# Small tables loaded already transposed by element-wise transfers, in a one-core hybrid encoder layer

## What is computed

```
mod = jax.nn.silu(c) @ w_ada + b_ada
sh1, sc1, g1, sh2, sc2, g2 = jnp.split(mod[:, None, :], 6, axis=-1)
mix, state = mixer(x * (1.0 + sc1) + sh1)
x = layer_norm(DEEPNORM_ALPHA * x + g1 * mix, ln_g[0], ln_b[0])
ffn = moe_ffn(x * (1.0 + sc2) + sh2, w_router, b_router, w_e_in, b_e_in, w_e_out, b_e_out)
x = layer_norm(DEEPNORM_ALPHA * x + g2 * ffn, ln_g[1], ln_b[1])
```

## Time and profile before

| | |
|---|---|
| three runs, median (lowest to highest) | 1493.74 us (1493.7 to 1495.0) |
| the profiled execution | 1493.7 us, span 1492.0 us |
| mean granted TensorE clock | 0.937 of full speed |
| busy share of the span | TensorE 88%, its weight loads 35%, VectorE 32%, ScalarE 15%, GpSimd 3% |
| moved from and to DRAM | 451.5 MB read, 3.8 MB written |

### The profile page before, as it was taken

The page is one execution under the profiler, slowest core; times in us unless marked ns, Lnnn a source line. Parts: engine busy times, 40 slices in busy tenths (PEclk is TensorE's granted clock), DMA queues, the critical chain, the costliest instruction groups (busy, mean ns, idle before and its releaser), DMA issues.

```text
span 1492.0 us, 20461 instructions
## 1 busy us (share of the span) xinstructions
PE 1315.2 (88%) x7752; PEld 520.1 (35%) x7753; DVE 478.3 (32%) x1190; ACT 218.1 (15%) x446; POOL 47.4 (3%) x78
## 2 busy tenths in 40 slices
PE   4797977719999999999899999999999999999992
PEld 1584333313333333333333333333333333333330
DVE  1383331662232233223322232223323232232237
ACT  0002111031111111110101101120110112112110
POOL 5300000020000000000000000000000000000000
PEclk9897976858999999999999999999999999999996
DMA  9910894338998699999999999959999996835050
GB/s 331 334 39 22 290 305 164 127 110 342 409 410 323 258 410 410 410 409 410 410 410 410 410 410 410 410 224 373 410 410 410 410 410 278 320 137 217 0 190 32
DMA packets 130789, 455.01 MB, mean 305 GB/s; under 512 B 14739, under 2 KB 20765, under 8 KB 130705
## 3 DMA queue, kind: packets, MB, share of 16 engines
q1 hardware_dynamic: 123376, 447.54, 76.9%
q10 hardware_dynamic: 7393, 7.22, 1.6%
HBM read 451.51 MB, written 3.79 MB: 305 GB/s over the span
## 4 chain that ended last, share of the span: by engine, by line
PE 60%; DMA 29%; DVE 5%; issue 3%; ACT 1%; ACTq 1%; SPq 1%; POOL 0%; DVEq 0%; POOLq 0%
DMA w<-in_w_e_out 27%; PE bank L1392 19%; PE bank L1355 19%; PE bank L1314 4%; PE bank L1135 4%; PE bank L1083 3%; PE bank L1267 2%; PE bank L1335 1%; PE bank L1183 1%; PE bank L1186 1%; PE bank L1120 1%; DMA w_odd<-in_w_ada 1%; DMA w<-in_state_conv 1%; PE bank L1377 1%; PE bank L1344 1%
## 5 line engine op out<-in xcount | busy, mean ns | idle before, releaser
L1392 PE MATMUL bank<-w,mt 128*64 128x512 f32 x1216 | 280.2, 615 | 38.7 <-DMA w<-in_w_e_out 38.7
L1355 PE MATMUL bank<-w_even,mt 128*64 128x512 f32 x1344 | 296.5, 594 | 7.9 <-ACT mt L651 7.9
L1355 PE MATMUL bank<-w_odd,mt 128*64 128x512 f32 x1088 | 239.2, 592 | 0.0
L996 DVE TENSOR_SCALAR mt<-bank 128x512 f32<-128x512 f32 x38 | 26.3, 692 | 593.4 <-PE bank L1355 593.4
L1392 PEld LDWEIGHTS bank<-w,mt 128*64 128x64 f32 x1216 | 87.9, 141 | 208.7 <-issue 164.7
L1355 PEld LDWEIGHTS bank<-w_even,mt 128*64 128x64 f32 x1344 | 94.9, 137 | 182.6 <-issue 180.9
L963 DVE TENSOR_TENSOR xy<-bank,xy 128x512 f32<-128x512 f32 (+1 forms) x234 | 146.1, 678 | 8.8 <-PE bank L1314 8.8
L1314 PE MATMUL bank<-mt,gpickT 64*128 64x512 f32 (+1 forms) x468 | 129.6, 631 | 0.7 <-ACT mt L665 0.7
L1355 PEld LDWEIGHTS bank<-w_odd,mt 128*64 128x64 f32 x1088 | 76.2, 137 | 140.2 <-issue 137.7
L1335 PE MATMUL bank<-pick,hb 128*128 128x64 bf16 x1824 | 70.0, 194 | 14.1 <-DVE gpick L991 14.1
L1335 PEld LDWEIGHTS bank<-pick,hb 128*128 128x128 bf16 x1824 | 65.5, 98 | 44.2 <-issue 30.0
(11 more groups left out here) (255 smaller groups left out, 872.5 us busy)
## 6 DMA issues: line engine op xcount, KB each, us to landing
w_even<-in_w_e_in SPq DMA_DIRECT2D x64, 2048.0 KB, 17.5
w<-in_w_e_out SPq DMA_DIRECT2D x64, 2048.0 KB, 18.3
w_odd<-in_w_e_in SPq DMA_DIRECT2D x64, 2048.0 KB, 19.6
w_odd<-in_w_ada SPq DMA_DIRECT2D x12, 2048.0 KB, 8.3
w_even<-in_w_in SPq DMA_DIRECT2D x2, 2048.0 KB, 23.5
w_even<-in_w_in SPq DMA_DIRECT2D x8, 256.0 KB, 5.0
w_even<-in_w_in SPq DMA_DIRECT2D x2, 1024.0 KB, 7.8
w<-in_w_out SPq DMA_DIRECT2D x4, 512.0 KB, 14.6
```

Source lines behind the costliest of these rows:

```text
L996: v.tensor_scalar(glu, bank[1][:, :], LIMIT, None, ALU.min).then_inc(m["glu"], 1)
L1355: ins = mm(bank[bk][64 * h:64 * h + 64, :], xT[:, SLOTS * k:SLOTS * (k + 1)], w1t[:, k, first + 512 * h:first + 512 * (h + 1)], start=Fals ...
L1392: ins = mm(bank[4][64 * h:64 * h + 64, :], aT[:, P * j + SLOTS * (k // 4):P * j + SLOTS * (k // 4) + SLOTS], w2t[:, k, 512 * h:512 * (h + ...
```

## The change

c is loaded directly as `cT` [128, 2, 8], with the model dimension on partitions; the bias tables are loaded as [4, 257] and [8, 32], with the heads on partitions; `conv_b` is loaded as `cbc` [128, 2] with a semaphore of its own. In each of these five transfers neighbouring destination elements are not neighbours in DRAM, so every 4-byte element is a run by itself: 1024 for each c, 1028, 256 and 256. The four TensorE transposes of c and of the tables and the four copies behind them go; GpSimd builds both extended tables from the loaded ones. In ScalarE's queue the two table loads now stand behind the loads of `cs`, `cbc` behind x, and the wait for c with the sigmoid behind the last of the DRAM-to-DRAM copies.

```diff
@@ tiles
-        crow = sb("crow", [2 * DK, P])
-        csil = sb("csil", [2 * DK, P])
+        cT = sb("cT", [P, 2, DK])
-        csig = sb("csig", [2 * DK, P])
+        csig = sb("csig", [P, 2, DK])
-        tabA = sb("tabA", [P, 2, AH])
-        tabB = sb("tabB", [T5_BUCKETS, BH])
-        tabBT = sb("tabBT", [BH, T5_BUCKETS])
+        tabA = sb("tabA", [AH, 2 * A_CLIP + 1])
+        tabB = sb("tabB", [BH, T5_BUCKETS])
+        cbc = sb("cbc", [P, 2])
@@ GpSimd
-            pool.wait_ge(tabB_ready, 1)
+            pool.wait_ge(ld["tabs"], 32)
+            g.tensor_copy(extA[:, 0:256], tabA[:, 0:1].to_broadcast([AH, 256])).then_inc(ext_done, 1)
+            g.tensor_copy(extA[:, 256:512], tabA[:, 0:256]).then_inc(ext_done, 1)
@@ ScalarE's queue
-            eng.dma_start(crow[0:DK, :], c_prompt[0].rearrange("(k p) -> k p", p=P)).then_inc(ld["c"], 16)
-            eng.dma_start(crow[DK:2 * DK, :], c_sample[0].rearrange("(k p) -> k p", p=P)).then_inc(ld["c"], 16)
-            eng.dma_start(tabA[:, :, :], rel_bias_a[0, 0:2 * A_CLIP].rearrange("(t p) h -> p t h", p=P)).then_inc(ld["tabs"], 16)
-            eng.dma_start(tabB[:, :], t5_bias).then_inc(ld["tabs"], 16)
+            eng.dma_start(cT[:, 0, :], c_prompt[0].rearrange("(k p) -> p k", p=P), allow_slow_non_contiguous=True).then_inc(ld["c"], 16)
+            eng.dma_start(cT[:, 1, :], c_sample[0].rearrange("(k p) -> p k", p=P), allow_slow_non_contiguous=True).then_inc(ld["c"], 16)
             eng.wait_ge(cs_zero, 1)
             eng.dma_start(cs[0:CONV_W, :], conv_w[0]).then_inc(ld["cs"], 16)
-            eng.dma_start(cs[CONV_W:CONV_W + 1, :], conv_b[0:1, :]).then_inc(ld["cs"], 16)
             eng.dma_start(cs[32:32 + PADW, :], state_conv[0, 0]).then_inc(ld["cs"], 16)
-            eng.wait_ge(ld["c"], 32)
-            a.activation(csig[:, :], crow[:, :], ACT.Sigmoid).then_inc(csig_done, 1)
+            eng.dma_start(tabA[:, :], rel_bias_a[0].rearrange("r h -> h r"), allow_slow_non_contiguous=True).then_inc(ld["tabs"], 16)
+            eng.dma_start(tabB[:, :], t5_bias.rearrange("r h -> h r"), allow_slow_non_contiguous=True).then_inc(ld["tabs"], 16)
             eng.dma_start(ka_c, cache_a_k[0, 0].rearrange("(t p) h d -> p t (h d)", p=P)).then_inc(ld["ka"], 16)
...
+            eng.dma_start(cbc[:, :], conv_b[0].rearrange("(k p) -> p k", p=P), allow_slow_non_contiguous=True).then_inc(ld["cb"], 16)
...
+            eng.wait_ge(ld["c"], 32)
+            a.activation(csig[:, :, :], cT[:, :, :], ACT.Sigmoid).then_inc(csig_done, 1)
 
             eng.wait_ge(ext_done, 2 + len(t5_runs()))
@@ VectorE
             dve.wait_ge(csig_done, 1)
-            v.tensor_tensor(csil[:, :], crow[:, :], csig[:, :], ALU.mult).then_inc(csil_done, 1)
-            dve.wait_ge(c_turned, 1)
-            v.tensor_copy(scT[:, :, :].rearrange("p k g -> p g k"), bank[4][:, 0:2 * DK].rearrange("p (g k) -> p g k", g=2)).then_inc(scT_done, 1)
-            dve.wait_ge(tabs_turned, 1)
...
+            v.tensor_tensor(scT[:, :, :].rearrange("p k g -> p g k"), cT[:, :, :], csig[:, :, :], ALU.mult).then_inc(scT_done, 1)
@@ TensorE
             pe.wait_ge(consts_done, 2)
-            pe.wait_ge(csil_done, 1)
-            nc.tensor.transpose(bank[4][:, 0:2 * DK], csil[:, :], ident[0:2 * DK, 0:2 * DK]).then_inc(c_turned, 1)
-            pe.wait_ge(ld["tabs"], 32)
-            for t in range(2):
-                nc.tensor.transpose(bank[5][0:AH, P * t:P * (t + 1)], tabA[:, t, :], ident[:, :])
-            nc.tensor.transpose(bank[5][0:BH, 256:256 + T5_BUCKETS], tabB[:, :], ident[0:T5_BUCKETS, 0:T5_BUCKETS]).then_inc(tabs_turned, 1)
-            pe.wait_ge(ld["cs"], 48)
+            pe.wait_ge(ld["cs"], 32)
```

More of the change, by code:

```diff
@@ L189, in hybrid_streaming_encoder_step @@
         ld = {n: sem(f"ld_{n}") for n in (
-            "c", "x", "cs", "ka", "kb", "v", "tabs", "cln", "sinks", "be", "wr", "ext", "toep", "wout",
+            "c", "x", "cs", "ka", "kb", "v", "tabs", "cb", "cln", "sinks", "be", "wr", "ext", "toep", "wout",
             "brow", "final", "x1s")}
@@ L202, in hybrid_streaming_encoder_step @@
             sem(n) for n in ("consts_done", "b3_done", "ext_done", "masks_done", "cs_zero"))
-        csig_done, csil_done, c_turned, scT_done = sem("csig_done"), sem("csil_done"), sem("c_turned"), sem("scT_done")
-        tabs_turned, tabB_ready = sem("tabs_turned"), sem("tabB_ready")
+        csig_done, scT_done = sem("csig_done"), sem("scT_done")
         ada_done, mod_ready = sem("ada_done"), sem("mod_ready")
@@ L420, in _ @@
                    allow_small_or_imprecise_dtypes=True).then_inc(consts_done, 1)
+            extA = MT[0:AH, 0:EXT]
             extB = MT[0:BH, EXT:2 * EXT]
-            pool.wait_ge(tabB_ready, 1)
+            pool.wait_ge(ld["tabs"], 32)
+            g.tensor_copy(extA[:, 0:256], tabA[:, 0:1].to_broadcast([AH, 256])).then_inc(ext_done, 1)
+            g.tensor_copy(extA[:, 256:512], tabA[:, 0:256]).then_inc(ext_done, 1)
             for a, b, bk in t5_runs():
-                g.tensor_copy(extB[:, a:b], tabBT[:, bk:bk + 1].to_broadcast([BH, b - a])).then_inc(ext_done, 1)
+                g.tensor_copy(extB[:, a:b], tabB[:, bk:bk + 1].to_broadcast([BH, b - a])).then_inc(ext_done, 1)
             g.memset(uext[:, :, 0:PADW], 0.0).then_inc(masks_done, 1)
@@ L709, in _ @@
             pv = ps[:, 0:128].rearrange("p (c w) -> p c w", c=2)
-            link(v.tensor_copy(cwT[:, :, :], pv[:, :, 0:32]))
+            link(v.tensor_copy(cwT[:, :, 0:CONV_W], pv[:, :, 0:CONV_W]))
             v.tensor_copy(uext[:, :, U_S:U_S + PADW], pv[:, :, 32:32 + PADW]).then_inc(tr_used, 1)
@@ L757, in _ @@
             dve.wait_ge(masks_done, 1)
+            dve.wait_ge(ld["cb"], 16)
             for c in range(2):
@@ L764, in _ @@
             for c in range(2):
-                link(v.tensor_scalar(yconv[:, c, :], uext[:, c, 0:Y_LEN], cwT[:, c, 0:1], cwT[:, c, CONV_W:CONV_W + 1], ALU.mult, ALU.add))
+                link(v.tensor_scalar(yconv[:, c, :], uext[:, c, 0:Y_LEN], cwT[:, c, 0:1], cbc[:, c:c + 1], ALU.mult, ALU.add))
                 for w in range(1, CONV_W):
```

## The result

| | before | after |
|---|---|---|
| median (lowest to highest) | 1494.25 us (1493.7 to 1495.0), 4 runs | 1511.38 us (1510.74 to 1512.0), 4 runs |
| span of the profiled execution | 1492.0 us | 1511.2 us |
| mean granted TensorE clock | 0.937 | 0.935 |
| DMA packets on ScalarE's queue (q10) | 7393 | 10687 |

The ratio is 1.0114, 95% interval [1.01, 1.0129]: 17.1 us slower, where 1513 was predicted, with 1508 to 1519 as the forecast's own range and 1500 to 1526 for 8 in 10. The bytes moved are the same, 455.01 MB; q10 has 3294 packets more.

What follows compares the result with a forecast made beforehand. Unit 0's start was taken to bound the kernel: hold until 20, 14.5 us of transfers, then sigmoid and product put unit 0 at about 37.5 against 17.50, +20 on 1493.7: 1513.7, say 1513; range 1508 to 1519, 8 in 10 1500 to 1526.

Steps and rivals of the forecast that it cites:

- What sets the start: Start of the kernel: unit 0's start sets everything behind it; a late start isn't caught up in the expert loop.
- The sigmoid's place: ScalarE's queue: sigmoid, at 6.60 before, comes behind all transfers; near 24 by order alone, near 36 in all.
- Depth of about 80 packets per DMA engine: DMA queues: an instruction is held until what was issued before it is down to about 80 packets per engine.
- Spread of `tabA` over four engines: Load of tabA: four rows of 257 elements likely go to four engines, 257 each; evenly spread, 64 each.
- Pace of a packet: Small packets on ScalarE's queue: 19.6 ns apiece alone, taken from 256-byte packets; one for one beside SyncE's unit loads.
- the 281: Small packets left of 338 on the fullest engine after units 0 and 1 load: 5.5 us at 19.6 ns.
- rival of dear packets: Small packets on ScalarE's queue: a 4-byte element costs more than 19.6 ns, +25 us and more; chance 0.23.
- From there to the sigmoid: ScalarE's queue after tabB's issue: 26 transfers take 14.5 us, from 20 to 34.5; sigmoid near 36.1 after its table load.
- VectorE's product: Between sigmoid and unit 0: VectorE's product takes 0.28 us, on the way to unit 0 at about 37.5.
- Unit 0 to unit 3: From unit 0 to unit 3's data: 21.2 us before, taken as even within 1.5 us.
- The clock: Granted TensorE clock, 0.81 in the starting stage: taken as even.
- the end of the hold: ScalarE's queue: one long hold at or behind tabB's issue, ending near 20.

Runs made afterwards that it cites:

- the spread table: Changed kernel with rel_bias_a loaded over 128 partitions in 1024 4-byte elements, tile unused, kind A's biases left out: 1510.09 us, ratio 1.0099.
- the kernel where GpSimd waits: Changed kernel with one more wait: GpSimd begins splitting the expert biases only when scT is done: 1511.78 us, ratio 1.0105.
- the last group: Third of three groups of experiments, each timed beside the kernel before on the same chip; that kernel's median there was 1495.48 us (27 runs).

## Why the prediction was right, step by step

- **What sets the start**: right. Unit 0's start, and behind it units 2, 3 and `w_in`, moved everything; the expert loop gave nothing back.
- **The sigmoid's place**: right, and the largest part. Moved alone it costs 8.3 us.
- **Depth of about 80 packets per DMA engine**: right at the first hold, 82; wrong at the second, which was released with 67 packets left in all, 17 on each of four engines. What the prediction didn't say is where the first hold would stand: at `conv_w`, for 8.86 us. It asked for one hold; there are two.
- **Spread of `tabA` over four engines**: right, shown by the spread table and by the quarter of the pace.
- **Pace of a packet**: the mis-sized term. 19.6 ns was taken from 256-byte packets; 4-byte ones take 11.2 ns at most, and 7.3 to 7.8 where they can be seen by themselves. By 11.2 the 281 take 3.1 us, not 5.5, and with the prediction's own sum the hold would end at 17.5; it ended at 17.8 instead of 20. The agreement is in part chance, since the depth was wrong as well and 0.8 us passed with no packet on q10. The rival of dear packets falls.
- **From there to the sigmoid**: 17.81 to 31.53 is 13.7 us, where 14.5 was taken; the sigmoid began at 32.85 instead of near 36.
- **VectorE's product**: taken at 0.28, it took 1.72 beside GpSimd. This was missed. Unit 0 came at 35.8, 1.7 before the forecast.
- **Unit 0 to unit 3**: taken as even, it gave back 2.2 us (19.05 against 21.2). Why is open. It isn't that x and the others had been moved in the gap: with the sigmoid late in the kernel before they had been too, and there it took 22.1 us (28.59 to 50.68). The traces differ in the Toeplitz reads. In the changed kernel q10 passes nothing from 44 to 50 us, while q1 passes 615 packets; there, from 38 to 48 us, it is 812 beside 814. No run tests this.
- **The clock**: taken as even; in the two profiled executions it was not. The first 6 us of the projections and 7 us in attention, before (from 225) and then after (from 244); the last row is the first 6 us of the projections in the kernel where GpSimd waits. Columns as in the earlier trace rows.

```profile
54.67:60.67 6.00, 6.00 (x18) 4.57 (x19) 0.00 (x0) 0.23 (x1) 0.00 (x0) 0.73 1.14 227
225.00:232.00 7.00, 4.61 (x30) 2.19 (x30) 1.68 (x7) 1.19 (x3) 0.00 (x0) 0.74 1.02 408
```

```profile
70.79:76.79 6.00, 6.00 (x13) 4.24 (x14) 0.00 (x0) 0.00 (x0) 0.00 (x0) 0.51 1.21 262
244.00:251.00 7.00, 4.61 (x24) 2.14 (x22) 1.68 (x7) 1.19 (x3) 0.00 (x0) 0.50 1.03 410
```

```profile
70.94:76.94 6.00, 6.00 (x18) 4.49 (x19) 0.00 (x0) 0.28 (x1) 0.00 (x0) 0.74 1.10 266
```

In the same stretch TensorE is just as busy and gets through fewer instructions, 13 instead of 18 and 24 instead of 30: the granted clock is 0.51 and 0.50 instead of 0.73 and 0.74, the 1.2 GHz of its two levels (1.2 and 2.4) for longer. Before that, while VectorE wrote `hT`, TensorE was busy for less than half of the time in both late kernels (from 62 us to 70.94, 3.81 us in the changed one and 3.53 in the third). The third kernel starts its projections as late as the changed one, at 70.94, and lost nothing. From the second part of the projections (line 1120) to the output projection four other kernels took 142.0 to 142.1 us as the kernel before did, and seven 143.2 to 143.6 as the changed one did, among them all that start sooner than the kernel before. So this term belongs to the execution; that the change causes it isn't shown.

In the profiled executions the output projection is 18.9 us late (268.0 against 249.1) where the projections were 16.1 late. Against +20, three terms were too large (the end of the hold, 20 for 17.8; 14.5 for 13.7; the distance to unit 3, 2.2), and two were missed (the product's 1.4 us and the 2.8 between the two shifts, which go with the clock): 20 - 2.2 - 0.8 - 2.2 + 1.4 + 2.8 = 19.0, about the 19.2 by which the profiled spans differ (1511.2 - 1492.0). The medians differ by 17.1, nearer to the projections' 16.1; the 27 executions of the kernel before in the last group lie 5.2 us apart (1492.69 to 1497.9), so one pair of profiles can't settle 2 us. That the forecast came within 2 us of the median is partly luck, since errors of both signs cancelled.

## To carry to other kernels

Before turning a row load into an element-wise one, count packets, not bytes: on the fullest DMA engine, beside what streams on the other queue, and ask which instruction of the issuing engine is held and what compute stands behind it in program order. Look at the outermost extent of a small load as well: with 4 rows of 257 elements four DMA engines carried it and the queue was held for 6.16 us, with as many elements spread over 128 partitions for 2.02. And a bound found by delaying something is only a bound in that direction: to gain from it, look up the next wait first.

## What the runs showed of the hardware

- Element-wise 4-byte packets pass at 7.3 to 7.8 ns each per DMA engine when the other queue is idle (876 on four engines in 1.6 us, 1633 on sixteen in 0.8), faster than 256-byte ones (19.6 ns), but about one for one with the other queue's packets when it isn't (735 against 813 in 10.88 us).
- A hold behind loads that lie on all 16 engines ended with 71 to 83 packets left on each (82 behind c). Behind the load on four engines it ended with 67 left in all, 17 on each if they lie evenly, after 0.8 us without a packet.
- Holds appear one instruction behind their cause, and a later hold absorbs an earlier one (8.86 + 6.16 us became 13.99).
- A VectorE product of 16 elements on 128 partitions took 1.72 us beside a GpSimd `tensor_tensor` and 0.17 without it; both ended together (34.90 and 34.86).
- Weights issued 2.3 us sooner were awaited until the same moment, 49.66 us: 10.9 us instead of 8.6. Up to 42 us their queue passed no packet, while the other passed 907 in 4 us.
